# Scan inputs: three token turns moved one or two products later, two sigmoids moved forward on ScalarE

## The reference, cut to what matters

```python
h = rms_norm(x, norm_g[layer]) * (1.0 + scale) + shift
proj = h @ w_in[layer]
(hq, hf, hi, hz, rq, rk, rv, rz, ga, gb) = jnp.split(proj, offsets, axis=-1)
# in the scan:
q = jax.nn.silu(q)
f = lbh + (1.0 - lbh) * jax.nn.sigmoid(fpre)      # fpre is hf
k = 1.0 - f
logf = jnp.log(f)
```

## Time and profile before

| | |
|---|---|
| median of 3 runs | 2670.04 us (2668.05 to 2671.69) |
| profiled execution, its own time | 2670.99 us |
| its span, first to last instruction | 2669.2 us |
| mean granted TensorE clock | 0.992 |
| busy share of the span: PE, PEld, DVE, ACT, POOL | 97%, 81%, 62%, 32%, 42% |

### The profile page before, as it was taken

How to read it: one execution, slowest core, us unless ns; L and a number is a source line. 1 busy time by engine, 2 the same in 40 slices (tenths; PEclk the granted TensorE clock), 3 DMA queues, 4 the chain that set the end, 5 groups by cost and what they waited for, 6 DMA issues and landing times.

```text
span 2669.2 us, 33144 instructions
## 1 busy us (share of the span) xinstructions
PE 2591.1 (97%) x13218; PEld 2174.4 (81%) x13218; DVE 1659.6 (62%) x2194; ACT 844.0 (32%) x1332; POOL 1131.9 (42%) x651
## 2 busy tenths in 40 slices
PE   6999899989999999999999999999999999999998
PEld 5788788877788777888888887888888888888887
DVE  4879978766512587666674558804555556476566
ACT  4011233334223433333332436212222222343342
POOL 2433100046632548777754444673223322242364
PEclk9999999999999999999999999999999999999999
DMA  4122333235312412222245553573333342466682
GB/s 153 56 94 97 99 124 127 95 104 206 112 62 79 158 58 86 79 87 79 87 149 191 169 178 121 186 258 106 134 111 111 130 147 94 159 251 211 223 315 111
DMA packets 147381, 360.25 MB, mean 135 GB/s; under 512 B 15173, under 2 KB 51229, under 8 KB 147100
## 3 DMA queue, kind: packets, MB, share of 16 engines
q1 hardware_dynamic: 65072, 177.81, 19.9%
q10 hardware_dynamic: 82156, 180.33, 18.9%
HBM read 268.90 MB, written 89.19 MB: 134 GB/s over the span
## 4 chain that ended last, share of the span: by engine, by line
PE 89%; DVE 4%; POOL 2%; ACT 2%; issue 1%; DMA 1%; ACTq 0%; POOLq 0%; DVEq 0%
PE pp L296 32%; PE pp L2213 13%; PE pp L494 11%; PE pp L2266 9%; PE pp L278 9%; PE pp L2953 2%; PE pp L1272 2%; POOL w_lo L3653 1%; PE pp L1944 1%; PE pp L1983 1%; POOL w_hi L3651 1%; DMA w_raw<-in_weights 1%; PE pp L1558 1%; PE pp L1597 1%; PE pp L444 1%
## 5 line engine op out<-in xcount | busy, mean ns | idle before, releaser
L3651 POOL CAST w_hi<-w_raw 128x1024 fp32r<-128x1024 f32 x184 | 222.2, 1207 | 990.3 <-PE pp L296 659.5
L296 PE MATMUL pp<-w_hi,act_hi 128*128 128x512 f32 x1344 | 535.9, 399 | 12.7 <-POOL w_lo L3653 9.9
L296 PE MATMUL pp<-w_lo,act_hi 128*128 128x512 f32 x1344 | 524.5, 390 | 0.0
L296 PE MATMUL pp<-w_hi,act_lo 128*128 128x512 f32 x1344 | 524.5, 390 | 0.0
L3653 POOL TENSOR_TENSOR w_lo<-w_raw,w_hi 128x1024 fp32r<-128x1024 f32 x184 | 468.9, 2549 | 14.7
L296 PEld LDWEIGHTS pp<-w_hi,act_hi 128*128 128x128 f32 x1344 | 253.0, 188 | 67.9 <-POOL w_lo L3653 10.8
L296 PEld LDWEIGHTS pp<-w_hi,act_lo 128*128 128x128 f32 x1344 | 252.6, 188 | 53.5
L296 PEld LDWEIGHTS pp<-w_lo,act_hi 128*128 128x128 f32 x1344 | 253.2, 188 | 48.3
L494 PE MATMUL pp<-act_hi,w_hi 128*128 128x512 f32 x480 | 192.7, 402 | 10.6 <-DVE act_lo L849 6.5
L2184 POOL TENSOR_TENSOR w_lo<-w_raw,w_hi 128x1024 fp32r<-128x1024 f32 x52 | 132.5, 2550 | 164.7 <-ACT w_hi L2178 164.6
L494 PE MATMUL pp<-act_lo,w_hi 128*128 128x512 f32 x480 | 190.5, 397 | 0.0
(11 more groups left out here) (468 smaller groups left out, 5282.9 us busy)
## 6 DMA issues: line engine op xcount, KB each, us to landing
w_raw<-in_weights SPq DMA_DIRECT2D x314, 512.0 KB, 3.5
z_s<-hg_st ACTq DMA_DIRECT2D x52, 512.0 KB, 4.1
hid_s<-ffn_cb ACTq DMA_DIRECT2D x22, 512.0 KB, 2.6
ffn_graw<-hid_s ACTq DMA_DIRECT2D x44, 256.0 KB, 3.1
hg_qkb<-hT_s SPq DMA_DIRECT2D x16, 512.0 KB, 8.1
qkvT_s<-mixin_o ACTq DMA_DIRECT2D x12, 512.0 KB, 2.8
gdn_qkv<-qkvT_s ACTq DMA_DIRECT2D x8, 768.0 KB, 6.4
front_x<-in_x ACTq DMA_DIRECT2D x8, 512.0 KB, 5.0
```

The lines of the kernel that those rows point to most:

```text
L296: last = pe.matmul(dst, a[:, k, t * P:(t + 1) * P], columns(w, j, k, 0, n), start=(k == 0 and a is high and w is w_hi), stop=(k == NK - 1 ...
L3651: pool.tensor_copy(hi, raw).then_inc(w_split, 1)
```

## The change

On TensorE, the turn of tile 5 moves from behind product 2 to behind product 3, that of tile 6 from behind product 3 to behind product 4, and that of tile 7 from behind product 3 to behind product 5. On ScalarE the sigmoid of product 2 moves from behind the third strip's casts to right behind the sigmoid of product 1, ahead of `high` of tile 5; the sigmoid of product 3 moves from behind `high` of tile 7 to ahead of `high` of tile 6. VectorE, GpSimd and SyncE keep their lists.

```diff
--- before.py
+++ after.py
@@ -2652,7 +2652,7 @@
                     self.made.done(product_half(pe, strip, m % 2, self.dst(j), h, frees=(m % 2 == 0)), "tile")
                     if j == 1:
                         self.prev.released(pe)
-                    for t in {1: (4,), 2: (5,), 3: (6, 7)}.get(j, ()):
+                    for t in {1: (4,), 3: (5,), 4: (6,), 5: (7,)}.get(j, ()):
                         R.turn(pe, t)
 
             def act(self, act):
@@ -2673,14 +2673,14 @@
                 R.high(act, 4)
                 R.second(act, 6)
                 sig(1)
+                sig(2)
                 R.high(act, 5)
                 R.second(act, 7)
                 self.prev.cast_down(act, N_DOWN * 2 + 4)
                 self.prev.cast_down(act, N_DOWN * 2 + 5)
-                sig(2)
+                sig(3)
                 R.high(act, 6)
                 R.high(act, 7)
-                sig(3)
                 self.prev.cast_down(act, N_DOWN * 2 + 6)
                 self.prev.cast_down(act, N_DOWN * 2 + 7)
```

## The result

The changed kernel takes 2684.93 us (median of 4 runs, 2682.56 to 2687.53) against 2670.6 for the kernel before (4 runs, 2668.05 to 2671.69). The ratio is 1.0061, with a 95% interval of 1.0048 to 1.0073: slower by 16.3 us, between 12.8 and 19.5. The two medians by themselves lie 14.3 apart, which is inside that interval too.

What follows compares the result with a forecast made beforehand. TensorE was taken as the bound, product 4 waiting for the third strip's low parts. Product 6 14.5 us later plus products 6 and 7 2.5 longer made 17.0, so a median of 2687.0; eight in ten 2680 to 2693.

Steps and rivals of the forecast that it cites:

- What bounds: TensorE ahead of product 4: bound by turn of tile 5, high 5, second 7, casts, low parts; 11.83 us.
- Turn of tile 5: Turn moved behind product 3: ScalarE's casts and GpSimd's low parts shift along, product 4 starts 5.44 us later, at 1650.78.
- The fourth strip: Ahead of product 6: strip ready 8.07 us after tile 7's turn starts, product 6 at about 1673.2, TensorE idle about 7.3.
- The clock: TensorE behind each of the two gaps: the clock falls to 1.2 GHz and costs 2.51 us each time.
- Half of the throttled time: Skill's rule for the clock penalty: 3.75 us per stretch, 7.5 for two gaps instead of 5.0, time 2689.5.
- What lies behind: TensorE from product 4 to 1803 us: no later stage absorbs the loss; two covers shrink without binding.
- The fifth strip: On GpSimd ahead of product 8: its margin goes from 2.3 to 4.8 us, as product 6 runs slow.
- the margin of the first silu ahead of product 24: First silu done before product 24 needs it: margin shrinks from 19.7 us to about 15.
- The scan inputs' chain: On VectorE after `low` of tile 7: shifts from 1647.28 to about 1669.3, 22 us against TensorE's 17.
- Only the first gap: Rival, 5%: fourth strip ready when tile 7's turn ends, product 6 only 7.2 us later, no second clock drop: 2677.3.
- Faster: Rival, 3%: the weights don't bind, product 4 right behind tile 5's turn, product 6 starts 6.2 us earlier: 2663.8.
- a longer loss: Rival, 10%: slower low parts, longer low clock and a late raw half add 6.4 us: 2693.

Runs made afterwards that it cites:

- Run 3: The changed kernel with the turns of tiles 5 and 6 put back, only tile 7's late: 2678.47 us against 2668.49 for the kernel before, ratio 1.0038.
- run 5: The changed kernel with the casts of both the third and fourth strips moved earlier on ScalarE: 2663.83 us against 2667.95 for the kernel before, ratio 0.9985.
- run 8: The changed kernel with the third strip's casts ahead of `second` of tile 7: 2681.86 us against 2667.41 for the kernel before, ratio 1.0052.
- run 4: The changed kernel with the fourth strip's casts ahead of `high` of tile 7: 2676.82 us against 2668.49 for the kernel before, ratio 1.0032.
- run 9: As run 5, but the third strip's casts behind the sigmoids of products 1 and 2: 2665.1 us against 2667.41 for the kernel before, ratio 0.9987.
- run 7: The kernel before, turns and sigmoids unmoved, with only the third strip's casts behind `second` of tile 6: 2670.21 us against 2667.95, ratio 1.0006.

## Why the prediction was right

**What bounds.** That product 4 waits for the third strip's low parts and not for `normalise` of tile 7 was read from 0.10 us between two rows. Run 3 shows it: with tile 7 out of the way product 4 came at the same distance. Runs 5 and 8 show the chain's links: move the casts, and product 4 moves with them.

**Turn of tile 5.** Product 4 was forecast 5.44 later. Counted from tile 4's turn it came 5.40 later (23.57 against 18.17), and 11.79 behind the turn of tile 5 against 11.83.

**The fourth strip.** 8.17 us from tile 7's turn to product 6 was the forecast (8.07 and 0.1), 8.10 the measurement, with 4.83 for the pair against 4.91.

**The clock.** This is the term that was off: 2.51 for each of two slow stretches. Product 4 up to the turn behind it shows 1654.22 - 1647.13 - 5.44 = 1.65, products 6 and 7 show 1682.23 - 1668.65 - 10.88 = 2.70. Together that is 4.35 instead of 5.02. With the 0.04 and 0.07 above it makes 16.2 out of 17.0, and 16.2 is what the stage shows. That the sum of the clock came so near is in part luck: one stretch cost less than charged and the other more, and over all profiles a stretch had 5 to 14 slow matmuls.

**Half of the throttled time.** The Trainium skill (TensorE: Matmul & The Clock Gate, "HAM oscillation — how this bites in real kernels") takes half of the throttled time for the penalty, and the prediction made an estimated 2689.5 of that. The trace agrees with the page only for the throttled time in which matmuls run. With two levels of the clock, the windows above give it: at mean 0.77 over 7.09 us and 0.62 over 7.35 us, 3.3 and 5.6 us were at the lower level, half of which is 1.6 and 2.8, beside 1.65 and 2.70 paid. The gaps, at 0.67, hold another 7.1 and 4.7 us of low clock that cost nothing, since TensorE had nothing to do; counted with them, the half would be 5.2 and 5.1. The 3.75 in the prediction also took all of a stretch of 7.5 us at 0.54 as throttled; its own working for the range has 3.45.

**What lies behind.** Nothing absorbed the loss: from product 6 to the end of the stage TensorE showed no further wait, and the time from the last silu to the end of the span was 867.8 us against 868.8. The fifth strip was ready 4.4 us ahead of product 8 (forecast 4.8).

One step here was wrong, though it cost nothing in this kernel: the margin of the first silu ahead of product 24 was to shrink from 19.7 to about 15, and it shrank to 9.2 (the silu done at 1760.06, product 24 at 1769.27). The scan inputs' chain began 20.6 us later from tile 4's turn, near the 22 forecast, but the first silu came 26.7 later. The prediction had the chain only shifted; VectorE's instructions in it (L2746, L2748, L2751 and L2758) were busy for 87.5 us instead of 78.5. Why they took longer was not tested. With the fourth strip's casts early the margin is 3.7 (runs 4 and 5), and in run 9 it is gone, which is the wait of 1.0 us there. So the fastest version stands close to the next wait.

**The median** came out at 2684.93 against a forecast of 2687.0. Against the kernel before the loss is 14.3 by the medians of 4 runs each and 16.3 by the ratio; the forecast 17.0 lies in the interval.

**The rivals.** "Only the first gap" needed the fourth strip ready in time; run 4 built that case and measured +8.5 (forecast 7.2). "Faster" needed both strips ready; run 5 built that one. Of "a longer loss" no term came: the pairs took 5.97 and 4.83 us, the two slow stretches cost less than charged in sum, and the fourth strip's casts ran without a wait for a raw half.

## What to carry to other kernels

When a step is moved later in one engine's list, look at what stands behind its consumer on the other engines. Here the step's own result was not wanted for four products, but ScalarE's next job in the list, a cast for a weight strip, was. Taking a wait away pays only when the next wait at the same place goes too. Here that one was named by the row that ends 0.1 us before the engine resumes, and not by the larger wait beside it. And check the covers further on: a chain that is only delayed can also come out longer, as the one to the first silu did.

## What the runs showed of the hardware

The price of a fallen clock did not grow with the length of the gap. Behind gaps of 2.21, 2.76 and 4.46 us there were 12, 10 and 12 slow matmuls; behind gaps of 6.90 to 7.65 there were 5, 8, 8, 10, 13 and 13; behind gaps of about 10.8 there were 7 and 14. At 0.2 us each that is 1.0 to 2.8 us. In run 7 the eight transposes behind the gap ran slow too and were on the path: 1.62 us from tile 7's turn to product 4 instead of 0.79. Each count is from one execution; what sets it is open. The gap of 1.41 us in run 9 was followed by no slow matmul.

GpSimd's subtraction (L2184) and VectorE's instructions took longer side by side. VectorE's on 128x1024 took about 3.24 us instead of 1.23 or 1.28, and GpSimd's pair 5.7 to 6.1 beside them instead of 4.66 where VectorE was idle for most of it. It is not only VectorE's instructions with two tensors to read: in the changed kernel L2746 and L2748, with one, took 2.10 and 2.44 us beside the fourth strip's pair, and 0.54 and 0.43 later, where GpSimd was idle.

Identical lists ahead of the stage put its start anywhere in 8.4 us (1621.67 to 1630.02) from one execution to the next, more than half of the effect under study. A difference of two spans would have been read as 11.6 us.
